# The C matrix of the state-space layer loaded and prepared later in a decoder trunk kernel

## The reference

```python
for i in range(DEPTH):                      # DEPTH = 2
    mod = (silu(c) @ ada_w[i] + ada_b[i])   # 6 parts: shift, scale, gate, twice
    h = rms_norm(x, norm1_g[i]) * (1 + sc1) + sh1
    mix = dilated_attention(h, ...) if i == 0 else s5_mixer(h, ...)
    x = x + g1 * mix
    h = rms_norm(x, norm2_g[i]) * (1 + sc2) + sh2
    x = x + g2 * conv_ffn(h, ...)
return rms_norm(x, final_norm_g)

# s5_mixer, the part that matters here (lb = exp(a * step), coef = (lb - 1) / a, b, c complex)
bb = coef * b
x_t = lb * x_(t-1) + bb u_t
y_t = Re(c x_t)
```

## Time and profile before

| | |
|---|---|
| three runs | 2732.66, 2733.81 (median), 2735.42 us |
| the profiled execution | 2732.6 us, its span 2730.6 us, so 2.0 us lie outside the span |
| TensorE busy | 2658.2 us (97% of the span), granted clock 0.99 of full speed |
| VectorE busy | 2303.9 us (84%) |
| ScalarE busy | 1291.1 us (47%) |
| GpSimd busy | 519.4 us (19%) |
| DMA | 725.45 MB, mean 266 GB/s, 388 and 385 GB/s in the first two of 40 slices of the span |
| start of the first pass on TensorE | 61.73 us |
| start of the second pass on TensorE | 150.82 us |

### The profile page before, as it was taken

How to read it: one execution, slowest core, us unless ns; L and a number is a source line. 1 busy time by engine, 2 the same in 40 slices (tenths; PEclk the granted TensorE clock), 3 DMA queues, 4 the chain that set the end, 5 groups by cost and what they waited for, 6 DMA issues and landing times.

```text
span 2730.6 us, 50020 instructions
## 1 busy us (share of the span) xinstructions
PE 2658.2 (97%) x18412; PEld 2375.5 (87%) x18412; DVE 2303.9 (84%) x3390; ACT 1291.1 (47%) x1852; POOL 519.4 (19%) x466
## 2 busy tenths in 40 slices
PE   5999999999999999999999999999999999999998
PEld 2998888888898888888889999999788888888887
DVE  7978988888889999899999989998898975677755
ACT  2444444444434555435555344444365553455542
POOL 4242211101132111000111322244311110011122
PEclk8999999999999999999999999999999999999999
DMA  9989988889876887678888967779777766656663
GB/s 388 385 269 339 347 312 333 318 313 336 312 228 234 297 281 250 204 247 312 280 283 270 376 221 239 235 254 330 258 253 241 257 184 188 196 187 189 182 189 109
DMA packets 241978, 725.45 MB, mean 266 GB/s; under 512 B 51074, under 2 KB 60034, under 8 KB 240898
## 3 DMA queue, kind: packets, MB, share of 16 engines
q1 hardware_dynamic: 185184, 666.98, 71.1%
q10 hardware_dynamic: 56612, 56.01, 6.4%
HBM read 701.66 MB, written 25.44 MB: 266 GB/s over the span
## 4 chain that ended last, share of the span: by engine, by line
PE 83%; DVE 5%; POOL 1%; issue 1%; DMA 1%; ACT 1%; ACTq 0%; POOLq 0%; DVEq 0%
PE proj L1910 39%; PE proj L1913 22%; PE proj L1933 5%; PE proj L1934 4%; PE proj L1935 4%; PE proj L1915 3%; PE proj L1928 1%; DVE w_lo L1181 1%; PE proj L1931 1%; PE ps L2049 1%; PE ps L2139 1%; ACT w_hi L600 1%; DVE ada L1071 0%; DVE work L1115 0%; DVE work L1463 0%
## 5 line engine op out<-in xcount | busy, mean ns | idle before, releaser
L600 ACT ACTIVATE w_hi<-raw 128x1024 fp32r<-128x1024 f32 (+1 forms) x896 | 934.6, 1046 | 999.4 <-PE proj L1913 362.2
L1181 DVE TENSOR_TENSOR w_lo<-raw,w_hi 128x1024 fp32r<-128x1024 f32 (+1 forms) x896 | 1104.8, 1236 | 285.9 <-ACT w_hi L600 275.7
L1910 PE MATMUL proj<-h_hl,w_hi 128*128 128x512 f32 x3990 | 1007.5, 393 | 2.7 <-DVE x L1510 1.8
L1910 PEld LDWEIGHTS proj<-h_hl,w_hi 128*128 128x128 f32 x3990 | 730.5, 189 | 139.3 <-DVE x L1510 2.1
L1913 PEld LDWEIGHTS proj<-h_hl,w_lo 128*128 128x128 f32 x4256 | 580.6, 190 | 41.6
L1913 PE MATMUL proj<-h_hl,w_lo 128*128 128x256 f32 x4256 | 593.4, 282 | 0.0
L1071 DVE SCALAR_TENSOR_TENSOR ada<-ada,held 128x1024 f32<-128x1024 f32 x304 | 396.0, 1303 | 0.0
L1813 POOL TENSOR_TENSOR a_hl<-work,a_hl 128x256 fp32r<-128x256 f32 (+1 forms) x88 | 120.6, 1371 | 1137.3 <-ACT a_hl L880 1137.3
L1933 PE MATMUL proj<-a_hl,w_hi 128*128 128x256 f32 x864 | 245.6, 284 | 0.7 <-DVE a_hl L1401 0.6
L1934 PE MATMUL proj<-a_hl,w_hi 128*128 128x256 f32 x864 | 244.5, 283 | 0.0
L1935 PE MATMUL proj<-a_hl,w_lo 128*128 128x256 f32 x864 | 244.5, 283 | 0.0
(11 more groups left out here) (273 smaller groups left out, 2870.3 us busy)
## 6 DMA issues: line engine op xcount, KB each, us to landing
raw<-in_w_up SPq DMA_DIRECT2D x352, 512.0 KB, 4.9
ada<-in_ada_t SPq DMA_DIRECT2D x304, 512.0 KB, 5.7
raw<-in_w_in SPq DMA_DIRECT2D x224, 512.0 KB, 6.5
raw<-in_w_down SPq DMA_DIRECT2D x128, 448.0 KB, 3.5
raw<-in_w_down SPq DMA_DIRECT2D x64, 512.0 KB, 3.6
ada<-in_ada_w SPq DMA_DIRECT2D x48, 512.0 KB, 8.6
raw<-in_w_out SPq DMA_DIRECT2D x32, 512.0 KB, 5.1
raw<-in_ssm_w_in SPq DMA_DIRECT2D x32, 512.0 KB, 4.9
```

What stands on the lines that cost most here:

```text
L600: nc.scalar.activation(w_hi[:, j % LAG, 0:nk * P], raw[:, j % s.ring, 0:nk * P], ACT.Copy).then_inc(hi_ready, 1)
L1181: V.tensor_tensor(w_lo[:, j % LAG, 0:nk * P], raw[:, j % s.ring, 0:nk * P], w_hi[:, j % LAG, 0:nk * P].bitcast(F32), ALU.subtract).then_in ...
L1910: ins = mm(both, w_hi[:, j % LAG, w], hl[:, k].rearrange("p c t -> p (c t)"), start=(k == 0), stop=False)
```

## The change

The load of `c_raw` leaves the constants and becomes a step of ScalarE behind piece 23 of the first pass, with a semaphore of its own (`c_raw_in`); three waits for the constants now count nine. GpSimd makes its factor tables first and prepares C behind them. The scratch tiles of the preparation move from the ring `raw` to a region that is free by then, so the waits of SP and VectorE for `prep_done` go, and GpSimd waits for `mod_ready` instead. `store_cw` stays where it is.

```diff
--- before.py
+++ after.py
@@ -292,8 +292,8 @@
         t4b, o = cut(a_flat, o, TILES, 4)
         prep, o = cut(a_flat, o, 14, TILES)
         acc_spare = raw[:, RAW - 1, :]
-        t16a, _ = cut(raw_flat, (RAW - 1) * MODW, TILES, SC)
-        t16b, _ = cut(raw_flat, (RAW - 2) * MODW, TILES, SC)
+        t16a, o = cut(a_flat, 0, TILES, SC)
+        t16b, _ = cut(a_flat, o, TILES, SC)
         early = [cut(h_flat, (KT + 4 * n) * T, MODW)[0] for n in range(4)]
         early += [cut(a_flat, 0, MODW)[0]] + [ada[:, n, :] for n in range(ADA)]
         partial = [cut(work, o, T)[0] for o in (3584, 3840, 4096, 4352, 4608, 4864, 3072, 5120, 5376, 2048, 2304, 2560,
@@ -407,6 +407,7 @@
         lam_made, lam_turned, lam_copied, lam_out, lamr_out = (
             sem("lam_made"), sem("lam_turned"), sem("lam_copied"), sem("lam_out"), sem("lamr_out"))
         scale_made, c_in, prep_in, first_link = sem("scale_made"), sem("c_in"), sem("prep_in"), sem("first_link")
+        c_raw_in = sem("c_raw_in")
         early_in = [sem(f"early_in{s}") for s in range(EARLY)]
         first_in = [sem(f"first_in{s}") for s in range(ADA)]
         early_added, early_summed = sem("early_added"), sem("early_summed")
@@ -519,7 +520,6 @@
                     n = s.number(i, j)
                     if name == "qkv0" and j < s.ring:
                         sp.wait_ge(ada_summed, 2 * KT)
-                        wait(sp, prep_done, j // 6)
                     ahead = s.tight if isinstance(i, int) and i == 0 and j < s.ring else s.ring
                     wait(sp, lo_ready, n - ahead + 1)
                     sp.dma_start(raw[:, j % s.ring, 0:nk * P], src(i, blk)[:, k0 * P:(k0 + nk) * P]).then_inc(
@@ -584,13 +584,12 @@
                              (gains, a["gains"]), (slopes, a["slopes"]), (own, a["own"]),
                              (not_first, a["not_first"]), (dskip, a["ssm_d"]), (lane, a["lane"])):
                 act.dma_start(dst[:], src).then_inc(consts_in, 16)
-            act.dma_start(c_raw, a["ssm_c"]).then_inc(consts_in, 16)
             act.wait_ge(row_made, 1)
             act.dma_start(cs_d.unsqueeze(0), cs_first[0:1]).then_inc(row_stored, 16)
             act.wait_ge(x_in, 16)
             for k in range(KT):
                 nc.scalar.activation(squares[:, k, :], x[:, k, :], ACT.Square).then_inc(first_sq, 1)
-            act.wait_ge(consts_in, 16 * 10)
+            act.wait_ge(consts_in, 16 * 9)
 
             def high(s):
                 def f(i, j):
@@ -641,6 +640,10 @@
             def second_half(i):
 
                 norm(0, 0, 0, 8, 8)
+
+            def load_c_raw(i):
+
+                act.dma_start(c_raw, a["ssm_c"]).then_inc(c_raw_in, 16)
 
             def load_row():
 
@@ -737,6 +740,7 @@
             s = st["qkv0"]
             late = {b + 4: [hold(b)] for b in range(28)}
             late[28].append(second_half)
+            late.setdefault(23, []).append(load_c_raw)
             carry = run_steps(act, s.count, s.length, high(s), late, done=2, keep=True)
 
             s = st["qkv1"]
@@ -1182,8 +1186,6 @@
                                     w_hi[:, j % LAG, 0:nk * P].bitcast(F32), ALU.subtract).then_inc(lo_ready, 1)
                     if s.old and isinstance(i, int) and j in s.old:
                         k = s.old[j]
-                        if k == 0:
-                            dve.wait_ge(prep_done, 1)
                         dve.wait_ge(ada_in[k % ADA], 16 * (5 + k // ADA + 1))
                         add_piece(acc_spare, k % ADA, k, k)
                     for m in s.rows_at(i, j):
@@ -1297,7 +1299,7 @@
             dve.wait_ge(first_sq, KT)
             V.tensor_reduce(sumsq[:], squares.rearrange("p k t -> p t k"), AX.X, ALU.add).then_inc(first_sum, 1)
             dve.wait_ge(first_sum, 1)
-            dve.wait_ge(consts_in, 16 * 10)
+            dve.wait_ge(consts_in, 16 * 9)
             V.tensor_copy(hscale[:], gains[:, 0, :]).then_inc(coef_made, 1)
             take_first(0)
             inverse_root(0)
@@ -1720,13 +1722,6 @@
                 link(G.tensor_tensor(pr, m1, m2, ALU.subtract))
 
             pool.wait_ge(coef_made, 1)
-            cr, ci = c_raw[:, :, 0, :], c_raw[:, :, 1, :]
-            link(G.tensor_tensor(t16a, cr, wide(ncim, SC), ALU.mult))
-            link(G.tensor_tensor(t16b, ci, wide(cim, SC), ALU.mult))
-            link(G.tensor_tensor(cr, cr, wide(cre, SC), ALU.mult))
-            link(G.tensor_tensor(cr, cr, t16b, ALU.subtract))
-            link(G.tensor_tensor(ci, ci, wide(ncre, SC), ALU.mult))
-            G.tensor_tensor(ci, ci, t16a, ALU.add).then_inc(prep_done, 1)
             double(cos, sin)
             double(pr, pi)
             e_re, e_im = ef[:, 0, :, 0, :], ef[:, 0, :, 1, :]
@@ -1751,6 +1746,16 @@
             link(G.tensor_tensor(ef[:, 1, :, 1, :], e_re, nothing, ALU.add))
             link(G.tensor_tensor(ef[:, 2, :, 1, :], ef[:, 2, :, 0, :], nothing, ALU.add))
             G.tensor_tensor(ef[:, 3, :, 1, :], ef[:, 3, :, 0, :], nothing, ALU.add).then_inc(ef_made, 1)
+
+            pool.wait_ge(c_raw_in, 16)
+            pool.wait_ge(mod_ready, 4)
+            cr, ci = c_raw[:, :, 0, :], c_raw[:, :, 1, :]
+            link(G.tensor_tensor(t16a, cr, wide(ncim, SC), ALU.mult))
+            link(G.tensor_tensor(t16b, ci, wide(cim, SC), ALU.mult))
+            link(G.tensor_tensor(cr, cr, wide(cre, SC), ALU.mult))
+            link(G.tensor_tensor(cr, cr, t16b, ALU.subtract))
+            link(G.tensor_tensor(ci, ci, wide(ncre, SC), ALU.mult))
+            G.tensor_tensor(ci, ci, t16a, ALU.add).then_inc(prep_done, 1)
 
             def mix(i0, hl):
                 def f(i):
@@ -2004,7 +2009,7 @@
             for n in range(2 * KT):
                 q, k = divmod(n, KT)
                 if n == 18:
-                    pe.wait_ge(consts_in, 16 * 10)
+                    pe.wait_ge(consts_in, 16 * 9)
                     pe.wait_ge(lam_made, 1)
                     flat = lam.rearrange("p n j q r -> p (n j q r)")
                     for h in range(4):
```

## The result

The changed kernel took 2740.1 us (median of 9 runs, 2736.7 to 2743.0) against 2733.1 for the kernel before on the same chip: ratio 1.0022, 95% interval 1.0014 to 1.0031, slower by 3.8 to 8.5 us. A second measurement gave 2738.45 against 2734.30, ratio 1.0016 (1.0007 to 1.0024). The predicted 2735.7 was 4.4 too low; the time lies inside the range by 0.9. The profiled execution took 2741.5 us, span 2739.5, 8.9 more than the span before.

The account below looks back on a forecast made before the run. DMA (VectorE nearly full too) bounds the kernel to 88 us, TensorE from there. Gain -5.1, price +5.8, clock +1.2 sum to +1.9 us: 2735.7 us, range 2729.3 to 2741.

Parts of the forecast that it names:

- the range: Whole kernel: the measured time was to lie between 2729.3 and 2741 us, taking in A's middle and B's.
- the price: Second pass, around 185 us: waits for the late-prepared C cost TensorE 5.8 us, plus 1.2 us of slower clock.
- The gain: Before 88 us: 2.6 us from moved bytes plus 2.5 us from VectorE freed, 5.1 us; bounds 2.6 and 5.8.
- turns: GpSimd and VectorE operations alternate, each waiting out the other's: 1.93 or 2.37 us of GpSimd, 1.1 us of VectorE.
- rival C: First pass: VectorE is freed but the DMA doesn't follow; gain 2.6 alone, +4.4 us, 2738.2 us; chance 0.16.
- The clock: Second pass, behind stalls of 2.0 and 4.1 us: the clock may fall, costing 1.2 us; bounds nothing to 3.3.
- C's store: ScalarE's queue, second pass: issued at 199.5 us, lands 11.0 us later at 210.5, holding up the table stores.
- A: Second pass: turns hardly delay preparation or VectorE; price 0.6 net, no clock, -4.5 us, 2729.3 us; chance 0.22.
- B: ScalarE's store queue: first table store lands 9.7 us behind C's; price 10.7, +6.8 us, 2740.6 us; chance 0.17.
- the 2 us more of price: Second pass: extra price of about 2 us if softmax operations on VectorE took turns with GpSimd as well.
- the likeliest case: The prediction's own forecast, +1.9 us to 2735.7 us, with 2732.5 to 2739 for itself; chance 0.45.
- two ahead: ScalarE's store queue: an issue passes when the store two ahead of it has landed.

## Why the prediction was right or wrong

- **Direction and place: right.** The prepared C is what is waited for, by ScalarE at its store, and TensorE waits for the joins of pieces 13 and 14. With one of the six operations the price is gone. The preparation's length was 17.35 us against 17.8 worked out, ScalarE's wait 12.67 (10 to 14 asked for), the two stalls 1.52 and 3.94 us against 2.0 and 4.0, the stalls' sum +5.4 against +5.8.
- **The gain: the step that failed.** The prediction had 5.1 us, 2.6 of bytes and 2.5 of VectorE freed from turns; 1.7 arrived (1.3 to 2.6 in five executions). The first pass did begin 2.0 us sooner (59.75), and VectorE did run ahead as worked out (`w_lo` at 1.22 us from 64 to 88 us, the stall of 1.84 gone). The step from there to TensorE failed: "whatever is won ahead of 88 us is kept as long as VectorE and the DMA can run ahead of it". It left out ScalarE, whose hold frees TensorE's bank and stands in its list behind a `w_hi` that waits for a later piece's transfer. TensorE idled 2.25 us from 88 to 150 us for that. With VectorE alone freed nothing arrived (second pass at 150.88); with the holds one piece sooner 4.4 of the 5.1 us did, beside the same transfers. That there would be a wait for transfers at all was hidden by the mean share of 0.91 over 62 us, on which the prediction dismissed rival C. The same stretch of the kernel before in three parts (columns of the earlier trace rows):

```profile
88.00:110.00 22.00, 21.87 (x181) 21.53 (x180) 21.58 (x20) 9.42 (x15) 0.00 (x0) 1.00 1.03 408
110.00:130.00 20.00, 20.00 (x225) 19.84 (x224) 19.69 (x18) 8.88 (x15) 0.00 (x0) 1.00 0.99 393
130.00:150.00 20.00, 20.00 (x226) 19.85 (x225) 16.07 (x27) 11.41 (x21) 0.00 (x0) 1.00 0.70 227
```

  The DMA engines were full up to 130 us, and in the changed kernel `w_hi` waited there for its transfers, 2.51 us in the two rows shown above.
- **The clock: mis-sized.** 1.2 us taken, 3.4 in the profiled execution and 1.7 in its repeat. Behind the stall of 3.94 us the clock stood at 0.50 to 0.75 from 202 to 206 us. The prediction put no term behind piece 19, where in one execution it fell again to 0.51 and 0.63 for 4 us. Two stalls of 1.5 and 2.3 us left it at 1.00 in one kernel and brought it to 0.50 in another, so this term can't be had from the stalls alone.
- **C's store.** It was to land after 11.0 us as before, and landed after 5.4: with ScalarE waiting, no raw slot came free, and the DMA engines stood still for 4 us ahead of it. The changed kernel's stretch from 194 to 198 us, columns of the earlier trace rows:

```profile
194.00:198.00 4.00, 2.52 (x22) 2.32 (x20) 3.22 (x4) 0.24 (x1) 3.18 (x2) 1.00 0.00 0
```

  The table store behind it then took 14.3 us (12.5 in the earlier trace rows), beside the weights that had to be caught up. The two errors cancelled: the third table issue ended at 216.66 (216.6 predicted) and piece 19 began at 220.94 (220.5).
- **The rivals.** A (turns light, 2729.3) is refuted by every row of the turns. B (+6.8 by the queue) gave nearly the measured number for another reason. Its sign came true, the first table store landed at 215.5, 12.8 us behind C's, but C's had landed 8 us sooner than B had it, and the third issue ended at 216.66, not at 221.5. C (+4.4) was nearest on the gain (2.6), and its sign, a second pass at 148 us or later, came true. Its reason, that the DMA doesn't follow, did not hold: with the DMA share at 0.94 from 88 to 150 us in both, the holds one piece sooner let TensorE keep 4.4 us. That the softmax runs beside GpSimd untouched held: 1.00 and 0.94 us for its long operations, 1.01 and 0.94 before. The Trainium skill ("SBUF — State Buffer", Who interferes with whom) says this of instructions with at most one SBUF input, outside the 2-port modes, and of `tensor_reduce`. The trace agrees, and the 2 us more of price that the prediction named for the case without this rule did not come.

By the test that the prediction set itself (stalls in 180 to 230 us near the shift at 150 us) it was wrong as a whole: +5.4 net of stalls against -1.7. That is +3.7, and the missing 3.4 is the clock. That 2740.1 lies inside the range is luck: the range's upper end was put there for B, which did not happen as described, and the likeliest case (2732.5 to 2739) missed it, though it holds the second measurement, 2738.45. What stays open is why the clock falls behind a stall in one execution and not in the next.

## What to carry to other kernels

Before work of GpSimd is moved to behind something, ask for its length there and not for when it was ready before: 12.8 us of slack work became 17.35 us on the path of an in-order ScalarE, whose wait starved TensorE and then the DMA. A gain on one engine counts only as far as every engine that hands work on follows, with the order of its list: look for a copy that frees a bank and stands behind a wait for something else. Whether that wait will bite is read from the DMA share in stretches of 20 us, not from a mean over 60. Where GpSimd works in long operations, keep it off the stretches in which many short VectorE operations are awaited; between two stretches where VectorE has slack it costs nearly nothing.

## What the runs showed of the hardware that was not expected

- The same store of 1024 KB landed in 5.4 to 6.0 us at 197 us with the DMA share at 0.00 ahead of it, in 11.0 us in the kernel before beside a share of 0.88, and in 20.1 us at 221 us beside a share of 1.04.
- The issue of the third table store ended just behind the landing of the first: 216.66 behind 201.17 + 14.3 = 215.5 in the changed kernel, 216.07 behind 198.02 + 17.3 = 215.3 with the store behind piece 17. The second issue of that latter kernel was held for 4.92 us, to 208.67, though C's store, two ahead of it, had landed at 197.61 + 6.0 = 203.6. So the prediction's "two ahead" is not the whole rule.
- VectorE's two-column operation on SBUF took 1.03 us instead of 0.17 beside GpSimd, and eight operations of 128x256 12.55 us instead of 3.25.
